# Two-layer generator kernel: six spread rows of layer 0 turned once and loaded over the partitions, flags read by group, one modulation row of layer 1 moved into layer 0

## The reference

```python
for i in range(DEPTH):                                   # DEPTH = 2
    mod_l = (c_act @ mod_w[i] + mod_b[i]).reshape(b, 6, 1, d)      # six modulation rows, latents
    mod_c = (c_ctx_act @ mod_w[i] + mod_b[i]).reshape(6, d)        # the same for the context
    hl = modulate(rms_norm(xl, norm_g[i, 0]), mod_l[:, 0], mod_l[:, 1])
    ...                                                  # layer 0: conv and pooling mixer; layer 1: attention
    xl = xl + mod_l[:, 2] * yl
    h2l = modulate(rms_norm(xl, norm_g[i, 1]), mod_l[:, 3], mod_l[:, 4])
    ...                                                  # layer 0 does the same for the context
    y2 = moe(h2, router_w, router_b, moe_w_gate[i], moe_w_up[i], moe_w_down[i])
    xl = xl + mod_l[:, 5] * y2
```

## Time and profile before

| | |
|---|---|
| time, median of 3 runs | 918.53 us (918.35 to 922.79) |
| the profiled execution's own time | 919.13 us |
| its span, first to last instruction | 917.4 us |
| PE busy | 834.6 us (91%) |
| DVE busy | 399.8 us (44%) |
| ACT busy | 167.0 us (18%) |
| POOL busy | 157.2 us (17%) |
| read from HBM | 288.17 MB |
| mean granted TensorE clock | 0.981 |

### The profile page before, as it was taken

The page is one execution under the profiler, slowest core; times in us unless marked ns, Lnnn a source line. Parts: engine busy times, 40 slices in busy tenths (PEclk is TensorE's granted clock), DMA queues, the critical chain, the costliest instruction groups (busy, mean ns, idle before and its releaser), DMA issues.

```text
span 917.4 us, 10102 instructions
## 1 busy us (share of the span) xinstructions
PE 834.6 (91%) x3773; PEld 373.2 (41%) x3773; DVE 399.8 (44%) x829; ACT 167.0 (18%) x413; POOL 157.2 (17%) x185
## 2 busy tenths in 40 slices
PE   4899999999989999977978999979899999978785
PEld 2444445446733333322337544536546333322221
DVE  1369998316242233323143588457645122212110
ACT  2301012216200000000023111436612000000000
POOL 2100193121112022221012231320220100000000
PEclk9999999999999999999999999999999999999999
DMA  8999356625598999999989567621295999999994
GB/s 363 407 418 407 139 196 259 275 92 183 203 379 363 361 422 422 422 425 423 411 353 429 208 260 300 250 93 40 109 400 177 380 426 423 422 426 426 427 421 184
DMA packets 27879, 291.88 MB, mean 318 GB/s; under 512 B 5030, under 2 KB 5336, under 8 KB 9132
## 3 DMA queue, kind: packets, MB, share of 16 engines
q1 hardware_dynamic: 23472, 283.25, 75.4%
q0 software_dynamic: 4272, 7.80, 2.4%
q10 hardware_dynamic: 76, 0.02, 0.0%
HBM read 288.17 MB, written 8.91 MB: 324 GB/s over the span
## 4 chain that ended last, share of the span: by engine, by line
PE 60%; DMA 19%; DVE 13%; SPq 3%; ACT 2%; issue 2%; POOL 0%; DVEq 0%; POOLq 0%; ACTq 0%
PE bank L1364 19%; DVE WORK L2370 10%; PE bank L501 9%; DMA ring<-in_gu_pack 9%; PE bank L1389 8%; PE bank L1524 5%; DMA ring<-in_down_pack 4%; DMA ring<-in_win_pack 3%; PE bank L1226 3%; DMA ring<-in_mod_pack 2%; PE bank L1471 2%; PE bank L1307 1%; SPq L1025 1%; PE bank L558 1%; PE bank L1373 1%
## 5 line engine op out<-in xcount | busy, mean ns | idle before, releaser
L1364 PE MATMUL bank<-ring,hT 128*64 128x512 f32 x368 | 111.6, 609 | 6.0 <-DMA ring<-in_gu_pack 3.7
L1364 PE MATMUL bank<-ring,WORK 128*64 128x512 f32 x352 | 105.0, 612 | 11.4 <-DMA ring<-in_gu_pack 7.2
L2370 DVE SCALAR_TENSOR_TENSOR WORK<-WORK,par 128x512 f32<-128x512 f32 x116 | 90.7, 860 | 0.0
L501 PE MATMUL bank<-ring,hT 128*128 128x512 f32 (+2 forms) x256 | 88.0, 499 | 0.7 <-ACT hT L1641 0.7
L1389 PE MATMUL bank<-ring,WORK 128*64 128x512 f32 x384 | 86.8, 595 | 1.8 <-DMA ring<-in_down_pack 1.2
L2260 DVE SCALAR_TENSOR_TENSOR WORK<-WORK,bank 128x256 f32<-128x256 f32 x16 | 7.7, 481 | 137.6 <-ACT WORK L1678 137.6
L2260 DVE SCALAR_TENSOR_TENSOR hT<-hT,WORK,bank 128x256 f32<-128x256 f32 x18 | 8.6, 480 | 134.9 <-ACT hT L1678 128.2
L1683 ACT ACTIVATE WORK<-bank 128x256 f32<-128x256 f32 x34 | 13.1, 384 | 264.7 <-PE bank L1373 264.7
L501 PEld LDWEIGHTS bank<-ring,hT 128*128 128x128 f32 x256 | 46.0, 190 | 35.8 <-issue 34.0
L1471 PE MATMUL bank<-hT,ring 128*128 128x512 f32 x128 | 57.5, 609 | 1.8 <-DMA ring<-in_win_pack 1.8
L1524 PE MATMUL bank<-ring,B 128*128 128x512 f32 x128 | 56.6, 596 | 0.8 <-DVE B L2387 0.8
(11 more groups left out here) (346 smaller groups left out, 1209.7 us busy)
## 6 DMA issues: line engine op xcount, KB each, us to landing
ring<-in_gu_pack SPq DMA_DIRECT2D x41, 2048.0 KB, 15.8
ring<-in_mod_pack SPq DMA_DIRECT2D x24, 2048.0 KB, 12.2
ring<-in_down_pack SPq DMA_DIRECT2D x21, 2048.0 KB, 25.7
WORK<-in_gu_pack SPq DMA_DIRECT2D x5, 2048.0 KB, 17.6
ring<-in_wout_pack SPq DMA_DIRECT2D x4, 2048.0 KB, 12.0
ring<-in_win_pack SPq DMA_DIRECT2D x3, 2048.0 KB, 36.9
X<-in_gu_pack SPq DMA_DIRECT2D x3, 2048.0 KB, 8.6
B<-in_gu_pack SPq DMA_DIRECT2D x3, 2048.0 KB, 22.5
```

What stands on the lines that cost most here:

```text
L501: mm = pe.matmul(dst[:, 0:hi - lo], hT[:, k, t * P:(t + 1) * P], w[:, k, :], start=k == 0, stop=k == KC - 1)
L1364: mm = pe.matmul(dst[ST * x:ST * x + ST, :], HG[L][s][:, k, :], columns(units[x], 512 * k, 512), start=k == 0, stop=k == KC - 1)
L2370: ins = dve.scalar_tensor_tensor(out=acc, in0=src, scalar=w, in1=acc, op0=ALU.mult, op1=ALU.add)
```

## The change

It has five parts.

1. The two packs of layer 1's modulation row 1 are loaded before ("wout", 0, 1), in layer 0. PE does `mod_multiply(7)` right behind the layer norm's transposes, and `mod_turn(6)` and `mod_turn(7)` together behind piece 0 of the output projection. The two packs are no longer issued behind the reload of `X`.
2. The 48 products of `row_gates` and `moe_gates` go. In the middle of piece 4 of the output projection PE turns six columns into rows of 8 x 128 (`turn_gates`), ACT copies them to `GT`, stores them to DRAM with two DMAs and waits for the stores. POOL loads them back with six DMAs, each over 64 partitions, 64 x 1024 values, and DVE waits for all six (`spread_in`) before its expert loop.
3. PE reads one flag before the first expert step and one more at each later group, instead of eight after the first half step. DVE writes the flags a little sooner.
4. At the end of the experts of layer 0 PE uses the flag that it has. DVE counts the second tile's semaphore before the first tile's last product where there is no second tile.
5. `norm_rows("a1")` on DVE makes the first columns of `hT` before it scales the last tile, and PE turns all eight pieces of the first tiles at once.

```diff
 def stream_plan():
-    out += [("wout", 0, 0)] + pair(1, 0) + [("wout", 0, 1)]
+    out += [("wout", 0, 0)] + pair(1, 0) + pair(1, 1) + [("wout", 0, 1)]
     out += expert_units(0)
-    out += pair(1, 1)
...
             def mod_turn(i):
-                pe.wait_ge(sem("mod_rows"), i + 1)
+                pe.wait_ge(sem("mod_rows"), 8 if i >= 6 else i + 1)
...
+            def turn_gates():
+
+                pe.wait_ge(sem("mix_done"), 5)
+                cols = (gsc[:, 0, 1, :, 0], gsc_diff, mods[:, 0, 3, :, 0], shift_diff, mods[:, 0, 5, :, 0], gdiff)
                 for n, col in enumerate(cols):
+                    mm = pe.transpose(bank[n // 4][0:8, P * (n % 4):P * (n % 4) + P], col, ident)
+                mm.then_inc(sem("gate_mms"), 1)
...
                 if L == 0:
                     h_rows(range(4, 8))
-                    row_gates((1, 3, 4, 6))
...
+                if L == 0:
+                    pe.wait_ge(sem("onehot"), 1)
+                    two.append(second_tile(pe, 0, 0))
...
-                if L == 0:
-                    moe_gates((3, 4))
...
                 for u in range(STEPS):
                     g, q = divmod(u, 2)
+                    if c == 2 and q == 0 and g:
+                        two.append(second_tile(pe, 0, g))
                     gate_up(u, 0, (lambda: turn_hidden(u - 1, 0)) if u else lambda: slots(L))
-                    if u == 0 and c == 2:
-                        pe.wait_ge(sem("slots_ready"), L + 1)
-                        two = [second_tile(pe, L, g) for g in range(GROUPS)]
...
-            mod_turn(6)
+            mod_multiply(7)
...
+                    if i == 4 and k == 4:
+                        turn_gates()
...
                 mm.then_inc(sem("out_mm"), 1)
+                if i == 0:
+                    mod_turn(6)
+                    mod_turn(7)
...
-            turn_pair("a1", 0, range(4))
-            mod(7)
-            turn_pair("a1", 0, range(4, KC))
+            turn_pair("a1", 0, range(KC))
             turn_pair("a1", 1, range(KC))
...
+            mod_copy(7)
+            act.wait_ge(sem("gate_mms"), gates_before("r0") + 1)
+            act.activation(GT[:, 0:512], bank[0][0:8, :], ACT.Copy)
+            act.activation(GT[:, 512:768], bank[1][0:8, 0:256], ACT.Copy).then_inc(sem("gate_rows"), 1)
+            act.wait_ge(sem("gate_rows"), gates_before("r0") + 1)
+            for h in range(2):
+                act.dma_start(gd[h].rearrange("n (c f) -> c n f", c=4),
+                              GT[4 * h:4 * h + 4, :].rearrange("c (n f) -> c n f", n=6)).then_inc(sem("gates_stored"), 16)
+            act.wait_ge(sem("gates_stored"), 32)
             square_rows("m0", range(3))
...
                 if tag == "a1":
-                    for j in range(4):
+                    for j in range(3):
                         scaled(tag, j)
-                    mod_columns(7)
-                    norm_scale(1, 0)
+                    hcols(tag, 0, (1, 3))
+                    scaled(tag, 3)
+                    hcols(tag, 0, (5, 7))
+                    hcols(tag, 1, range(1, KC, 2))
+                    return
...
-                dve.wait_ge(sem("gate_rows"), gates_before(f"m{L}") + (2, 1)[L])
+                if L == 1:
+                    dve.wait_ge(sem("gate_rows"), gates_before("m1") + 1)
+                else:
+                    dve.wait_ge(sem("spread_in"), 96)
...
+            pool.wait_ge(sem("gates_stored"), 32)
+            pool.wait_ge(sem("x_added"), 8)
+            pool.wait_ge(sem("raw_scaled"), 1)
+            for n, dst in ((0, GB[:, 1, :]), (1, MR[:, :, :].rearrange("p a d -> p (a d)")), (2, GB[:, 0, :])):
+                for h in range(2):
+                    pool.dma_start(dst[ST * h:ST * h + ST], gd[h, 2 * n:2 * n + 2, :].rearrange("n d -> (n d)").partition_broadcast(ST))\
+                        .then_inc(sem("spread_in"), 16)
             experts(0)
```

More of the change, by code:

```diff
@@ L247, in generator_kernel @@
         xa = nc.dram_tensor("x_rows", (TOK, D), F32, kind="Internal").ap()
+        gd = nc.dram_tensor("spread_rows", (2, 6, 512), F32, kind="Internal").ap()
         HALVES = "t (h c) -> (t h) c"
@@ L386, in generator_kernel @@
         GM = [GB[:, 0, 512 * i:512 * i + 512] for i in (0, 1)]
+        GT = wk[0:8, 0:768]
         YP = wk[:, 0:2288].rearrange("p (m s t) -> p m s t", m=4, s=2)
@@ L412, in generator_kernel, with mod_at @@
         block = ctx.enter_context(nc.Block())
+        def mod_at(i):
+            return 16 * (i == 7)
         MOD_PAIRS = [u[1:3] for u in STREAM if u[0] == "mod" and u[3] == 0]
@@ L743, in moe_scalar @@
                 h_rows(range(2, 8))
-                for n, b in enumerate((1, 3, 4, 6)):
-                    act.wait_ge(sem("gate_mms"), gates_before("r0") + n + 1)
-                    act.activation(ROW_GATES[n], bank[b][:, :], ACT.Copy).then_inc(sem("gate_rows"), 1)
             for h in range(2):
@@ L1146, in products @@
                         mm.then_inc(sem("ln_turned"), 1)
-                for i in range(2):
-                    pe.wait_ge(sem(f"y_used_{i}"), GROUPS)
-                last = second_tile(pe, 0, GROUPS - 1)
-                with pe.If(last > 0):
+                with pe.If(two[GROUPS - 1] > 0):
+                    for i in range(2):
+                        pe.wait_ge(sem(f"y_used_{i}"), GROUPS)
                     products(2)
                 with pe.Else():
+                    for i in range(2):
+                        pe.wait_ge(sem(f"y_used_{i}"), GROUPS)
                     products(1)
@@ L1229, in project_out @@
                             sum_moe_rows()
+            two = []
             def route(L):
@@ L1367, in turn_hidden @@
                 def turn_hidden(u, s):
-                    if u == 0 and s == 0:
-                        pe.wait_ge(sem("gate_rows"), gates_before(f"m{L}") + (2, 1)[L])
+                    if L == 1 and u == 0:
+                        pe.wait_ge(sem("gate_rows"), gates_before("m1") + 1)
                     pe.wait_ge(sem(f"he_{s}"), U0 + u + 1)
@@ L1978, in mod_columns @@
                 r = R_MODB + 48 * L + 8 * v
-                dve.wait_ge(sem("mod_turned"), i + 1)
-                tt(mods[:, L, v, :, :].rearrange("p (h c) s -> p h c s", h=2), bank[7][:, 0:16].rearrange("p (c h s) -> p h c s", c=4, h=2),
+                dve.wait_ge(sem("mod_turned"), 8 if i >= 6 else i + 1)
+                tt(mods[:, L, v, :, :].rearrange("p (h c) s -> p h c s", h=2), bank[7][:, mod_at(i):mod_at(i) + 16].rearrange("p (c h s) -> p h c s", c=4, h=2),
                    par[:, r:r + 8].rearrange("p (h c) -> p h c", h=2).unsqueeze(3).to_broadcast([P, 2, 4, 2]), ALU.add).then_inc(sem("mod_cols"), 1)
@@ L2330, in experts @@
                             dve.nop()
-                if L == 0:
-                    last_places()
-                out_rows(GROUPS - 1, 0)
-                if c == 2:
-                    late_second(GROUPS - 1)
+                if L == 1:
+                    out_rows(GROUPS - 1, 0)
+                    return
+                last_places()
+                with dve.If(two[GROUPS - 1] > 0):
+                    out_rows(GROUPS - 1, 0)
+                    out_rows(GROUPS - 1, 1)
+                with dve.Else():
+                    bump(dve, [("y_used_1", 1)])
+                    link.n -= 2
+                    out_rows(GROUPS - 1, 0)
+                    bump(dve, [("vector_chain", 1)])
+                    link.n += 1
+                dve.nop()
             for j in range(4):
```

44 lines of the change are left out of this document (13 added, 31 removed).

## The result

The changed kernel takes 914.59 us (median of 9 runs, 911.16 to 917.94) against 921.18 us for the kernel before on the same chips (9 runs, 918.35 to 924.01). The ratio is 0.9933, 95% interval 0.9913 to 0.9952: it is faster by 0.67%, where the forecast of 906 to 918.53 us was 1.4%, and 914.59 us lies outside the forecast range of 902.5 to 911 us. The profiled execution took 915.22 us with a span of 913.6 us, 3.8 us less than the span before.

The account below looks back on a forecast made before the run. Prediction: full DMA bounds some stretches, chains of engine waits the others. Gains of 3.9 (experts, net of 3.65 added), 1.0 (last group) and 7.8 us (between layers) sum to 12.7: 919.13 to 906.4, said as 906; range 902.5 to 911.

Parts of the forecast that it names:

- Part A: Output projection of layer 0: added modulation product, turns and transposes make everything from its end on 3.65 us later.
- Part B, up to the hidden values: Start of layer 0's experts: without gate products and flag gap, hidden values turn near 253.5 us, PE 3.9 us ahead.
- spread rows late: Rival at VectorE's first hidden values: spread rows land up to 2 us late, 4 with slower issues; 908 to 910; chance 0.10.
- This gain must pass the DMA-bound stretch to count: Layer 0's experts: packs are issued earlier as PE frees slots, so the full DMA stretch ends earlier and 3.9 us survive.
- The order of slots freed is the same: Expert packs of layer 0: slots come free in the same order as before for every pack from the second group on.
- Part C: Last expert group of layer 0: only the wait on DVE's product remains before the spread, gaining 1.0 us (0 to 1.4).
- Part D: Between the layers: without the wait for a modulation pack, layer 1's projection gains 7.8 us (6.1 to 8.3).
- The rule on the flags: PE's flag reads: the skill's 600 ns floor makes single reads lose 4.2 us; the sum used the trace, which hides them.
- The gain is given back: Rival: packs ending the full DMA stretch in both layers land no earlier, issues hanging on something unseen; 915 to 918; chance 0.05.
- Slower: Rival at the experts' start: a long wait for spread rows eats the whole gain; 924 us and more; chance 0.04.
- the open flag reads: Rival in the experts: seven later flag reads at 0.67 us are not hidden, 4.7 us; 908 to 911; chance 0.08.
- another wait in front of layer 1's projection: Rival between the layers: the projection waits for something else, leaving a gain of 4 to 5 us; 909 to 911; chance 0.08.

Follow-up runs that it names:

- the second execution of the same program: The changed kernel with 48 empty instructions at the head of TensorE's program, which left the program as it is: 915.34 us, ratio 0.9954 to the kernel before.
- held packs: The changed kernel, with SyncE waiting for group 1's two gathers before issuing the third down pack and those behind it: 909.14 us, ratio 0.9888 to the kernel before.
- two loads: The changed kernel without four of its six loads of spread rows: 913.16 us, ratio 0.9933 to the kernel before.
- both remedies: The changed kernel with packs held until group 1's gathers land and 24 matmuls behind the second modulation product: 905.57 us, ratio 0.9845 to the kernel before.
- the kernel turned round: The changed kernel with packs held for group 1's gathers and the one-tile case first in the branch before the spread products: 908.68 us, ratio 0.9855.

## Why the prediction was wrong, point by point

**Part A** was right: 3.47 us for 3.65, and the stores and squares cost nothing. ACT's squares came at 198.03 for 198.2.

**Part B, up to the hidden values,** was right in each place and 0.5 us too good in sum: `gate_up` at 241.22, no gap, the turn at 254.11 for 253.5, because VectorE's first hidden step came at 253.12 and its second instruction ended at 254.05. Half a microsecond is less than two executions differ by, and this one has its own cause for it: its first gather took 8.30 us (granted clock 0.92 at 228.4 to 251 us) where the second execution of the same program has 7.31. The spread rows were in time: POOL's six issues took 0.52 to 0.63 us each, from 225.2 us on, the rows landed in 6.2 to 9.8 us, and no wait for them stands in the trace, as against rival "spread rows late".

**Part B, "This gain must pass the DMA-bound stretch to count",** is the step that failed. I looked for the stretch where DMA is full, 170 us later, and asked whether packs would be issued earlier. They were, and that did the damage, at its very beginning. I never asked what an earlier issue meets at 250 us: the gathers of group 1, which are tied to the routing and moved by only 0.4 us, while the packs moved by 4.2. The sentence "The order of slots freed is the same" was true, and did not bear on it, since the gathers are in POOL's queue. The price was 2.87 us of waiting and 1.70 us because the down products ran in part at 1.2 GHz (5.35 us for 3.65, granted clock 0.68), 4.57 in all, which turns a lead of 3.4 us into 1.2 us behind at 266.8 us; a further 0.9 us went until 463 us, for a cause that stays open. The pair of runs with held packs and with two loads shows that it is the packs and not the four loads left out; 4.1 us came back, and with both remedies 8.1. With the packs held the rest of that step of the prediction came true: the gain did pass the full stretch (reload of `X` 3.8 us sooner than before, for 3.9).

**Part C** failed too: +1.18 for -1.0. Of the 2.2 us between them, 1.7 stand behind VectorE's last product (2.13 us to the spread, where 1.41 less 1.0 was expected) and 0.5 in front of it (4.74 us from the reload for 4.28), which no run looked into. The step "With the change only the wait on the product is left" took a branch to be free. The branch moved to the front, as the diff has it, and there it took 4.43 us, of which 2.11 us showed behind the product. That it depends on the branch's place is shown (24 matmuls earlier in the program bring it to 0.21 us); that its target was not loaded is the reading that fits, since only the long branches have a load of instructions inside. The Trainium skill (Runtime: NRT & Kernel Launch, section Instruction fetch mechanics) says that a taken branch whose target lies outside the loaded pages has to fetch it by DMA before it goes on. The traces agree: 3.2 to 4.6 us in the seven kernels with such a load, 0.21 or 0.22 in six others, and 0.08 and 0.30 for the two branches of the kernel turned round. The page gives no price. With the place moved the spread starts 0.06 us behind the product, as forecast.

**Part D** was right: 7.66 us for 7.8. In the kernel with both remedies the projection starts at 477.78 us; the prediction had 476.7.

**The rule on the flags** was rightly left out of the sum. The Trainium skill (DMA: Bandwidth & Descriptors, section Latency and other measured facts) has some 600 ns for a register load, and by it, as an estimate, single reads lose 4.2 us. The traces have 0.31 us a read, and seven single reads show no gap at all; it was the seven in one go that opened 1.46 us.

**The rivals.** "The gain is given back" (chance 0.05, 915 to 918 us) comes nearest to the 914.6 us measured, but not where I put it: nothing hung on the end of the full stretch, the loss was at its beginning. "Slower" by late spread rows, the open flag reads and another wait in front of layer 1's projection did not come. Once the two losses were taken out the sum held within the interval: ratio 0.9845 (0.9826 to 0.9865) where 12.7 of 918.5 us are 0.9862. In the profiled execution of that kernel the projection came 11.6 us sooner than before, so some of the 14.3 us lies elsewhere and is not explained. One slip in the numbers: the chances of the rivals add up to 0.91, 0.05 and 0.04, where the prediction says 0.89, 0.06 and 0.05.

## What to carry to other kernels

When an engine gets faster, list what its progress sets free (here two 2 MB packs, 4 us sooner) and look at what small transfers are in flight then and did not move along; a gather that somebody waits for may need the packs held back, and if these packs have time to spare the hold costs nothing. A branch ahead of a wait is not free: look in the trace how long the branch itself took, and whether a load of instructions lies inside it. And a gain must be followed past the next thing that does not move with it, before it is followed to the end. Last, compare lengths within an execution before places between executions: two executions of one program put the same step up to 3 us apart here.

## What the runs showed of the hardware

- The four gathers that had landed in 2.5 to 3.7 us took 3.6 to 13.0 us once two packs of 2 MB were issued in their midst, at 249.6 and 250.0 us. With the packs held until three groups' gathers had landed, all six took 3.0 to 4.4 us.
- The branch's cost depends on where it stands in the program: 24 matmuls inserted 430 us earlier took it from 4.43 to 0.21 us. Breaks in the middle of the spread products (0.80 and 1.04 us) stood near a load of instructions in two kernels; that it caused them is not shown, and in the kernel with both remedies a load begins during these products without a break.
- A wait on TensorE can have a second price: after the wait of 2.87 us the next 16 products took 5.35 us in place of 3.65 (granted clock 0.68 over them, so 1.2 GHz for a part of it). The 16 spread products took 5.16 to 5.75 us behind gaps of 2.2 to 4.5 us and 3.70 us behind gaps of 0.86 and 1.71 us. The gap's length alone does not decide it: in the kernel before, 16 products behind a gap of 2.29 us took 3.65 us, at the full clock.
